# Cached keys scored four requests at a time, one 32-column strip each, in a decoder step on one Trainium2 core

## The reference, cut to what matters

```python
# window: the last 512 cached tokens
s = jnp.einsum('bqghd,bkgd->bqghk', qg, kr) * SCALE
# selected: 16 blocks of 64 cached tokens out of the paged cache (2048 tokens)
imp = jnp.where(current, FORCE, jnp.where(visible, imp, -FORCE))
_, idx = lax.top_k(imp, k)
s = jnp.einsum('bqghd,bgqkld->bqghkl', qg, kg) * SCALE
p = masked_softmax(s, mask)
o = jnp.einsum('bqghk,bkgd->bqghd', p, v)
```

## Time and profile before

| | |
|---|---|
| median of 3 runs | 2439.51 us |
| the profiled execution | 2438.98 us |
| its span | 2437.1 us |
| PE busy | 2388.9 us (98%) |
| DVE busy | 1474.5 us (61%) |
| ACT busy | 1071.9 us (44%) |
| POOL busy | 94.1 us (4%) |
| granted TensorE clock, mean | 0.994 |
| key units on PE, first to last | 324.3 to 433 us |
| `kbuf<-in_selk`, SP and POOL | 64 DMAs each, 192 KB each, 4.0 and 4.2 us to landing |

### The profile page before, as it was taken

How to read it: one execution, slowest core, us unless ns; L and a number is a source line. 1 busy time by engine, 2 the same in 40 slices (tenths; PEclk the granted TensorE clock), 3 DMA queues, 4 the chain that set the end, 5 groups by cost and what they waited for, 6 DMA issues and landing times.

```text
span 2437.1 us, 50797 instructions
## 1 busy us (share of the span) xinstructions
PE 2388.9 (98%) x20548; PEld 2258.7 (93%) x20548; DVE 1474.5 (61%) x1732; ACT 1071.9 (44%) x1302; POOL 94.1 (4%) x180
## 2 busy tenths in 40 slices
PE   8999998999999999999999999999999999999997
PEld 6888862779999999999999999999999999999996
DVE  6777778675866444444444778768754444444456
ACT  3333321454575353354353445446743534433433
POOL 0000014220000000000000010000000000000000
PEclk9999999999999999999999999999999999999998
DMA  9999669895555555555555564454555544454451
GB/s 377 352 327 325 213 202 319 303 332 224 186 188 214 199 213 200 211 202 183 205 178 184 174 227 172 169 175 173 173 188 174 186 176 181 180 181 181 179 184 70
DMA packets 102974, 516.80 MB, mean 212 GB/s; under 512 B 13088, under 2 KB 29536, under 8 KB 56640
## 3 DMA queue, kind: packets, MB, share of 16 engines
q1 hardware_dynamic: 91872, 467.90, 53.8%
q0 software_dynamic: 10976, 47.13, 5.6%
HBM read 508.59 MB, written 18.95 MB: 216 GB/s over the span
## 4 chain that ended last, share of the span: by engine, by line
PE 91%; DVE 4%; ACT 1%; issue 1%; DMA 1%; POOLq 0%; POOL 0%; SPq 0%; ACTq 0%; DVEq 0%
PE psa L441 28%; PE psa L442 27%; PE psa L443 27%; PE psm L477 2%; PE psa L645 1%; ACT whi L1100 1%; PE psm L841 1%; PE psa L820 1%; DVE page L1625 1%; DVE wlo L1609 1%; DVE stage L1835 1%; PE psa L638 1%; PE psm L672 1%; DMA page<-in_cmp 0%; PE psm L829 0%
## 5 line engine op out<-in xcount | busy, mean ns | idle before, releaser
L1609 DVE TENSOR_TENSOR wlo<-wraw,whi 128x2048 fp32r<-128x2048 f32 x356 | 815.7, 2291 | 770.3 <-ACT whi L1100 770.0
L1100 ACT ACTIVATE whi<-wraw 128x2048 fp32r<-128x2048 f32 x356 | 682.1, 1916 | 968.1 <-PE psa L443 962.1
L441 PE MATMUL psa<-xhi,whi 128*128 128x264 f32 (+1 forms) x2096 | 605.3, 289 | 13.7 <-DVE wlo L1609 12.0
L442 PE MATMUL psa<-xlo,whi 128*128 128x264 f32 (+1 forms) x2096 | 600.4, 286 | 0.0
L443 PE MATMUL psa<-xhi,wlo 128*128 128x264 f32 (+1 forms) x2096 | 599.0, 286 | 0.0
L443 PE MATMUL psa<-hhi,wlo 128*128 128x264 f32 x2048 | 581.4, 284 | 0.0
L442 PE MATMUL psa<-hlo,whi 128*128 128x264 f32 x2048 | 581.3, 284 | 0.0
L441 PE MATMUL psa<-hhi,whi 128*128 128x264 f32 x2048 | 580.8, 284 | 0.0
L443 PE MATMUL psa<-nhi,wlo 128*128 128x264 f32 x1536 | 435.2, 283 | 0.0
L442 PE MATMUL psa<-nlo,whi 128*128 128x264 f32 x1536 | 434.9, 283 | 0.0
L441 PE MATMUL psa<-nhi,whi 128*128 128x264 f32 x1536 | 434.9, 283 | 0.0
(11 more groups left out here) (424 smaller groups left out, 1565.2 us busy)
## 6 DMA issues: line engine op xcount, KB each, us to landing
wraw<-in_w SPq DMA_DIRECT2D x356, 1024.0 KB, 4.8
page<-in_cmp SPq DMA_DIRECT2D x128, 384.0 KB, 5.2
kbuf<-in_selk SPq DMA_DIRECT2D x64, 192.0 KB, 4.0
kbuf<-in_selk POOLq DMA_DIRECT2D x64, 192.0 KB, 4.2
vbuf<-in_selv SPq DMA_DIRECT2D x64, 192.0 KB, 4.2
vbuf<-in_selv POOLq DMA_DIRECT2D x64, 192.0 KB, 4.3
o_win<-in_win POOLq DMA_DIRECT2D x8, 1533.0 KB, 7.6
kbuf<-in_wink SPq DMA_DIRECT2D x8, 768.0 KB, 5.4
```

The costliest lines, as they stand in the source:

```text
L441: mm(out, wh, hi[:, k, 0:w], start=(k == 0), stop=False)
L442: mm(out, wh, lo[:, k, 0:w], start=False, stop=False)
L1100: A(whi[:, p % 2, :], wraw[:, p, :], ACT.Copy).then_inc(s.hi_ready, 1)
L1609: V.tensor_tensor(wlo[:, p % 2, :], wraw[:, p, :], whi[:, p % 2, :].bitcast(F32), ALU.subtract).then_inc(s.lo_ready, 1)
```

## The change

1. A key step `keys(j)` now takes four units at once, j = 0 to 9: unit 4j + n is request 2n + j % 2 and owns output rows 32n to 32n + 31. For each piece t four products with 32 output rows are issued, one per strip: 12 products in a step. `qzm` goes, `qzr` holds all three pieces. `k_used` rises at the four products of t = 2, so the four places come free together.
2. The rows of a finished bank are in another order. ACT copies the bank to `ktmp` (`rows_copy(c)`), PE multiplies it with a permutation matrix `perm` (`turn_keys(c)`, one product with 128 rows and 512 columns) back into the bank, and `bank_out(c)` waits for `k_turned` instead of `k_used`. The rows of the queries are put in the same order by three products with `perm` in place of three transposes (L600).
3. The ring has seven places for keys and values together: five in `kbuf`, two in `kmore`, over `tsam`. Its order runs through from keys to values; the last three value units go to places 3, 4 and 5, so that the weights of group 10 can be loaded over places 0 and 1 earlier.
4. The order on PE and ACT is written anew around it.

```diff
+        kmore = nc.alloc_sbuf_tensor_at("kmore", [128, 2, 4 * KW], F32, offset=base + a.at["tsam"])
+        VALUE0 = 40
+        def place(u):
+            return u % 7 if u < 77 else u - 74
+        def slot(u):
+            return kbuf[:, place(u), :] if place(u) < 5 else kmore[:, place(u) - 5, :]
+        def request(u):
+            return 2 * (u % 4) + u % 8 // 4
+        def before(u):
+            return max(v for v in range(u) if place(v) == place(u))
...
             for u in range(40):
                 if u < 5:
                     sp.wait_ge(s.lo_ready, 4 * (G_EOUT - 1) + (1, 2, 3, 3, 4)[u])
+                elif u < 7:
+                    sp.wait_ge(s.cmp_mm, 1)
+                    sp.wait_ge(s.rows_mm, 2)
+                    sp.wait_ge(s.stored, 16 * 6)
                 else:
-                    sp.wait_ge(s.k_used, u - 4)
+                    sp.wait_ge(s.k_used, before(u) + 1)
...
-                sp.wait_ge(s.v_used, 37 + p)
+                sp.wait_ge(s.v_used, (32, 33, 38, 39)[p])
                 weights(10, p)
...
-                pool.wait_ge(s.k_used, u - 4)
+                pool.wait_ge(s.k_used, before(u) + 1)
...
             for u in range(8, 40):
-                pool.wait_ge(s.v_used, u - 4)
+                pool.wait_ge(s.v_used, before(VALUE0 + u) - VALUE0 + 1)
...
-                        last = nc.tensor.transpose(psm[:, 0, 128 + 128 * t:256 + 128 * t], qflat[:, 128 * t:128 * t + 128], ident)
+                        last = mm(psm[:, 0, 128 + 128 * t:256 + 128 * t], qflat[:, 128 * t:128 * t + 128], C("perm"),
+                                  start=True, stop=True)
...
-            def keys(u):
+            def keys(j):
+                c, e = divmod(j, 2)
+                if j == 0:
                     pe.wait_ge(s.qz_done, 2)
+                if e == 0:
                     if c < 2:
                         pe.wait_ge(s.bank_free, 4 * (G_EOUT - 1) + c + 1)
                     else:
                         pe.wait_ge(s.k_evac, c - 1)
+                for t in range(3):
+                    for n in range(4):
+                        u = 4 * j + n
+                        if t == 0:
+                            pe.wait_ge(kin[place(u)], landed(u))
+                            if u >= 8:
+                                pe.wait_ge(kin_p[place(u)], landed_p(u))
+                        key = slot(u).rearrange("p (q t n) -> p q t n", q=4, t=3)
+                        ins = mm(psa[32 * n:32 * n + 32, c % 2, :], qzr[:, t, e, 32 * n:32 * n + 32], key[:, :, t, :],
+                                 start=(e == 0 and t == 0), stop=(e == 1 and t == 2), skip_group_check=True)
+                        if t == 2:
+                            ins.then_inc(s.k_used, 1)
+            def turn_keys(c):
+                pe.wait_ge(s.k_copied, c + 1)
+                mm(psa[:, c % 2, :], C("perm"), ktmp[:], start=True, stop=True).then_inc(s.k_turned, 1)
...
+                if g == 1:
+                    keys(2)
+                    turn_keys(0)
+            keys(3)
+            compressed_sums()
+            keys(4)
+            compressed_turn()
+            turn_keys(1)
+            turned_queries(0)
+            compressed_output()
+            keys(5)
+            pe.wait_ge(s.kv_rot, 2)
+            prompt_keys(0)
+            pe.wait_ge(s.gp_done, 1)
...
+            turn_keys(2)
+            keys(6)
...
-                    keys(next(key_units))
+                if g == 1:
+                    keys(7)
...
             for i in range(26):
-                if i < 4:
-                    keys(next(key_units))
+                if i in (0, 2):
+                    keys(8 + i // 2)
+                if i in (1, 3):
+                    turn_keys(3 + i // 2)
...
+            def rows_copy(c):
+                act.wait_ge(s.k_used, 8 * c + 8)
+                if c:
+                    act.wait_ge(s.k_turned, c)
+                A(ktmp[:], psa[:, c % 2, :], ACT.Copy).then_inc(s.k_copied, 1)
...
             def bank_out(c):
-                dve.wait_ge(s.k_used, 8 * c + 8)
+                dve.wait_ge(s.k_turned, c + 1)
```

More of the change, by code:

```diff
@@ L206, in part, with landed_p @@
             return g, kind, min(sub, 1), (0, 0, 2)[sub], (4, 2, 2)[sub]
-        def landed(u):
-            return 16 * sum(1 if v < 8 else 2 for v in range(u % 5, u + 1, 5))
+        VALUE0 = 40
[5 more added lines that the diff above has]
+            return 2 * (u % 4) + u % 8 // 4
+        def landed(u):
+            return 16 * sum(1 if v % VALUE0 < 8 else 2 for v in range(u + 1) if place(v) == place(u))
+        def landed_p(u):
+            return 32 * sum(1 for v in range(u + 1) if place(v) == place(u) and v % VALUE0 >= 8)
+        def before(u):
+            return max(v for v in range(u) if place(v) == place(u))
         o = Region(region_a, a_yacc)
@@ L769, in _ @@
             for g in range(KVH):
-                if g:
-                    keys(next(key_units))
                 if g < 3:
@@ L903, in _ @@
                     last.then_inc(s.conv_var, 1)
-                if i < 4:
-                    keys(next(key_units))
-                elif i < 24:
+                if 4 <= i < 24:
                     values(next(value_units))
@@ L1277, in _ @@
             for i in range(25):
+                if i in (0, 3):
+                    rows_copy(3 + i // 3)
                 if i >= 1:
```

166 lines of the change are left out of this document (59 added, 107 removed).

## The result

The changed kernel takes 2446.78 us, the median of 7 runs (2445.70 to 2448.12), against 2439.51 for the kernel before (7 runs beside it, 2436.49 to 2440.26): a ratio of 1.0034, 95% interval 1.0023 to 1.0045. It is slower by 0.34%, which is 8.3 us by the ratio; the two medians lie 7.3 us apart. The forecast was 2440.5 with a range up to 2449: the value lies in the range, 6.3 us above the forecast, and on the side of slower by over 0.2%, which had a chance of 0.29.

The account below looks back on a forecast made before the run. DVE's list of work in the attention stage, not PE, was taken as the bound. The terms 0.35 - 2.8 + 1.8 - 0.4 - 0.5 = -1.55 turned 2438.98 into 2440.5 us; range 2433 to 2449.

Parts of the forecast that it names:

- The chain to the exponential: PE's work up to ACT's exponential, through `keys(4)`: ends at 372.15, DVE wants it at 368.30 and loses 3.85 us.
- `bank_out(2)` without a wait: DVE's wait of 4.20 us for PE before this bank copy goes, because the bank is complete well before.
- Block outputs: `keys(7)` stands behind the fourth output at half clock, so the fifth output comes late: 2.8 us lost, 0.1 at full clock.
- the loop's first steps: `keys(8)`, `keys(9)` and the waits in `collect(0)` and `collect(1)`: 1.8 us gained, between -2.7 and 3.5.
- The tail: Last value units share the DMA engines with group 10's weights, released earlier: 0.5 us lost, between 0 and 3.
- `tri`: Table DVE waits for: earlier loading of units 5 and 6 may delay it 1 us, swallowed by the wait for the exponential.
- The slower one: Rival over the whole stage: the clock stays down and the ring holds DVE up, -8.95 us, 2447.9; chance 0.25.
- Its loop term: In the slower rival, `keys(8)` and `keys(9)` both run at half speed: 2.7 us lost.
- Its other half: In the slower rival, `keys(3)` also at half speed: exponential ends at 375.05, net 2.55 us lost with the `bank_out(2)` gain.
- its condition: The slower rival decides once `keys(3)` ends after about 356 us: the release, no longer POOL's queue, then sets the tempo.
- The reading that gaps of 1.2 to 1.8 us leave the clock alone: From the full-clock rival (2434.2, chance 0.20): in 362 to 378 such PE gaps kept the clock, only 2.89 lowered it.
- Strips overlap: Four 32-row products take 0.99 us together, a step 3.0; the rival without overlap, 6 us or more, 2448, chance 0.02.

Follow-up runs that it names:

- e1: The changed kernel with the compressed transpose, query transposes and compressed product moved ahead of `keys(4)`, its bank 1 permutation left behind it: 2444.52 us, ratio 1.0017.
- e3: The changed kernel with SP holding value units until the last key unit has landed, and group 10's weights until value units are nearly used: 2439.70 us, 1.0005.
- e5: The changed kernel with the edits of e1 and e3 together: 2436.99 us, ratio 0.9998 to the kernel before.
- e2: The changed kernel with identity products that nobody reads put into PE's gaps: 2443.42 us, ratio 1.0020 to the kernel before.
- e10: e9 with identity products behind the block outputs (28, then 5 each) and 14 ahead of `keys(9)`: 2437.16 us, ratio 1.0001 to the kernel before.
- e8: e4 with e3's two holds on SP added: ratio 1.0000 to the kernel before.
- e4: The kernel before with only the ring of seven places and its waits, keeping its old key products and order: ratio 1.0014 to the kernel before.
- e9: e5 with six DVE steps (two row products and their sums) moved ahead of the wait for `tri`: 2435.26 us, ratio 0.9987 to the kernel before.
- e12: The kernel before with only e9's six DVE steps moved ahead of the wait for `tri`: 2438.41 us, ratio 1.0001.

## Why the prediction was right or wrong

**In short.** The forecast was a loss of 1.6 us against a measured one of 9.0 between the profiles. The kernel was slower, the side the forecast was on, and the value is inside the range; the range was wide enough for it, and the size of the loss was not foreseen.

**The bound and the method held.** Nearly all of the loss stands as waits in DVE's list and on PE at the stage's end (6.6 and 2.15 of 9.0). PE's 12 us less made nothing faster, as the prediction had it.

**The chain to the exponential: size right, in part by luck, and one link wrong.** 3.86 against 3.85, and `bank_out(2)` without a wait; e1 removes the one by moving `keys(4)`. But `keys(4)` did not wait for a landing at 361.4. It waited for DVE to empty the first bank (362.10, released by DVE's L1865), a wait that the prediction does not have; that end and mine lay 0.7 apart by chance. In e1, where the bank was free at 361.63, the last unit landed at 363.83, so the landing is close behind. `keys(2)`, put at 3.0, took 6.09 near half clock and ended at 348.0 instead of 345.6. POOL did not issue at its own tempo over that, as I had said it would: it waited 2.82 us for the end of `keys(2)` and issued for the last unit of `keys(3)` at 348.40 instead of 346.05. `keys(3)` began at 353.28, forecast 352.2, straight behind PE's own block scores and without a wait for data. `keys(4)` took 6.9 us, forecast 5.7. The exponential ended at 373.6, not 372.15, and the wait was still 3.86, because DVE too came 1.4 us later (`cprod` and `tri`). e3, with 6.14 at this place, shows how much of the match is chance.

**Block outputs.** 2.18 against 2.8: `keys(7)` took 4.27 us, between the full and the half clock I had taken.

**The term that failed: the loop's first steps.** Forecast: `collect(0)` 12.7 us after M, the start of `mask_scores(0)`. Measured: 17.9 (M = 418.33). By links, forecast and measured: `keys(8)` ends at M + 1.1 and M + 2.7 (it began at M - 1.1, not at M - 2.8); release to POOL's first issue 0.25 and 1.3; its second 1.15 and 1.14; landing 5.0 and 6.57; `keys(9)` behind it 3.0 and 4.2; the rest 2.2 and 2.07. Four of six were too small, and the half clock is in two of them. `keys(8)` began late because the eighth block output and `scores(0)` ahead of it took 1.64 and 2.08 us at a clock of 0.50 (414 to 418), where the kernel before had 0.91 and 1.16. The other pair is the landing and what follows on it: SP's three value units of 768 KB, ordered at 423.3 to 424.7, slow the 192 KB that PE waits for, and PE, idle for 4.68 us, then takes 4.27 us for 18 records. e3 takes away the neighbours and gets 4.9 us back; e5 shows 3.28 and 2.73 for the two links. e2 lifts only the clock and gets 2.8 back, and e10, with both, has 2.52, hardly less than e3's 2.59. Why POOL's first issue took 1.3 us and not 0.25 is open. I had read the three ring places as space and not as traffic.

**The tail.** 2.15 against 0.5, within the 0 to 3 I gave. e3 and e8 remove it with the two holds on SP, e4 has it (2.83) without the strips. That the weights of group 10, let in early, do it is likely and not shown apart from the other hold.

**`tri`.** I saw the delay of 1 us and said the wait for the exponential would swallow it. It came as 1.02 and was added in full. A wait hides an earlier delay only if what is waited for does not itself follow the delayed engine. Here it did, since `keys(4)` followed DVE's copy-out. e4 and e8, with the ring alone, wait 2.77 and 2.85 us, so the delay comes with the ring; that units 5 and 6 make it is not shown. e9 lies 0.0011 (2.6 us, expected 1.5) under e5 with 1.58 us of the wait covered, a difference inside the intervals.

**The rivals.** The slower one gave 2447.9, near the result, and half of it came true. Its loop term, 2.7 lost with both steps at half clock, is near the 3.1 measured. Its other half did not: `keys(3)` ended at about 356, at the edge of its condition, and the exponential's net was what the forecast had and not 2.55 lost; `tri` and the tail made up for that. The clock did fall (0.53, 0.50); e2 gets 3.4 us back in the order as changed, e10 none in the repaired one, though its own products hide what a free full clock would give. The reading that gaps of 1.2 to 1.8 us leave the clock alone and only 2.89 brings it down does not hold in e4 and e8, where it fell behind 1.41 and 0.91. Strips overlap: a step at full clock takes 2.8 us (`keys(0)`: 2.78), even less than 3.0.

**What stays open.** Where e12's median execution loses its 1.5 us, and what the 2.5 us still waited in `collect(0)` at full clock are made of, and why the clock falls between the block outputs in e4 and e8. The hold on the value units and that on the weights were not tried apart; their 4.9 and 2.15 come from the ledger alone.

## What to carry to other kernels

When places or buffers come free together, list what every queue will order in that moment, largest first, and ask which of them the bound engine waits for; holding the others back until that one has landed (with the hold on the next weights) was worth 7 us here, moving one misplaced step 4, and both together the 8.3 that the change had lost. Follow each wait back to see whether it starts from the delayed engine before letting it hide a delay. And a gain on an engine that is not the bound is worth nothing until the transfers that it releases are known.

## What the runs showed of the hardware

- **Landing depends on the neighbours.** The same 192 KB DMA of POOL took 3.28 us with a DMA share of 0.47 (e5, 420 to 424) and 6.57 with 0.81 and 1.00 (the changed kernel, 424 to 428 and 428 to 432). Three profiles with SP's large transfers held back have 3.20 to 3.35, four without 6.08 to 6.57.
- **The same work can meet either clock.** The same stretch of the value loop, PE at the third group's values and outputs, in the kernel before:

```profile
451.44 1.50 PE L672 MATMUL psa<-vbuf,ptw 128*32 128x96 f32 x32
452.88 1.80 PE L841 MATMUL psm<-tok,ptp 128*128 128x96 f32 x8
```

and in e12:

```profile
448.70 0.87 PE L672 MATMUL psa<-vbuf,ptw 128*32 128x96 f32 x32
449.50 1.13 PE L841 MATMUL psm<-tok,ptp 128*128 128x96 f32 x8
```

The granted clock is 0.59 in the one (451 to 455) and 1.00 in the other (448 to 452); the idle time of PE just before is 1.39 us in both. DVE's wait there is 7.0 us or 5.5 us, with nothing between, in fourteen profiled executions of fourteen kernels: five times the long one. In the changed program and in e3, whose program is the same at this place, it is 7.02 and 5.51. Each kernel was profiled once, so whether one program meets both is likely and not shown. Runs of one program do differ in the clock: the kernel before took 2434.31 us with a mean granted clock of 0.997 and 2442.03 with 0.993, both in the set of e1 to e4. Of the 9.0 us between the profiles of before and after it is nothing, since both have the long one; between other pairs it is 1.5 us at a place that no edit touched.
